# Weighting and adding the early gathered expert rows on ScalarE and GpSimd, with half as many early steps more

## The reference

```python
best_s, sel = lax.top_k(cand_s..., PEER_TOPK)      # 16 of 256 candidates, 8 heads
gate = jax.nn.softmax(best_s, axis=-1)
act = jax.nn.gelu(jnp.einsum('thkd,td->thk', exp_u[idx], xb))
w = gate * act
return jnp.einsum('thk,thkd->td', w, exp_v[idx])
```

## Time and profile before

| | us |
|---|---|
| median of 3 runs | 3281.06 (3277.91 to 3286.41) |
| the profiled execution | 3273.5 |
| its span in the trace | 3271.7 |

### The profile page before, as it was taken

One profiled execution on the slowest core, in us unless ns is written; L12 is line 12 of the kernel. 1 busy time (PEld: TensorE's weight loads), 2 busy tenths in 40 slices (PEclk: granted clock), 3 DMA queues, 4 the chain that ended last, 5 costly groups with the idle time before them and its releaser, 6 DMA issues.

```text
span 3271.7 us, 46700 instructions
## 1 busy us (share of the span) xinstructions
PE 2966.7 (91%) x17310; PEld 2586.0 (79%) x17310; DVE 2489.2 (76%) x5433; ACT 808.7 (25%) x2386; POOL 1050.3 (32%) x840
## 2 busy tenths in 40 slices
PE   6898979999999999976878978789999999999876
PEld 5787868988888888865666856679888888888755
DVE  4277797888888888887543776888888888888876
ACT  3332222212111111211344353122121111111111
POOL 4542112333333333343255421123433323333331
PEclk9999989999999999988978978889999999999888
DMA  4336677899999999999421356668999999999994
GB/s 156 96 101 245 256 262 282 339 421 422 422 422 419 420 414 418 408 421 419 162 68 46 102 180 251 241 249 316 413 422 421 422 419 418 420 416 416 408 422 197
DMA packets 159967, 1042.99 MB, mean 319 GB/s; under 512 B 18480, under 2 KB 23920, under 8 KB 44096
## 3 DMA queue, kind: packets, MB, share of 16 engines
q0 software_dynamic: 92160, 671.13, 50.4%
q1 hardware_dynamic: 63648, 357.59, 28.1%
q10 hardware_dynamic: 4000, 12.36, 1.1%
HBM read 1033.28 MB, written 7.86 MB: 318 GB/s over the span
## 4 chain that ended last, share of the span: by engine, by line
DMA 42%; PE 37%; DVE 11%; issue 8%; ACT 1%; POOL 1%; SPq 0%; DVEq 0%; ACTq 0%; POOLq 0%
DMA gata<-uvg,idxg 25%; DMA gatb<-uvg,idxg 16%; PE bank L711 9%; PE bank L515 8%; DVE acc L1593 5%; PE bank L502 3%; PE bank L724 3%; PE bank L503 3%; PE bank L504 3%; PE bank L698 3%; PE bank L532 1%; PE bank L600 1%; PE bank L856 1%; DVE gata L1585 1%; DVE xf L1355 1%
## 5 line engine op out<-in xcount | busy, mean ns | idle before, releaser
L724 PE MATMUL bank<-a,V 128*128 128x256 f32 x4096 | 949.8, 392 | 100.2 <-DVE a L1576 100.2
L724 PEld LDWEIGHTS bank<-a,V 128*128 128x128 f32 x4096 | 806.8, 198 | 227.1 <-issue 109.9
L711 PE MATMUL bank<-xd,U 128*128 128x256 f32 x4096 | 939.1, 389 | 0.8 <-DMA U<-uvd 0.8
L1266 POOL DMA_INDIRECT gata<-uvg,idxg x428 | 521.6, 1219 | 1247.3 <-DVE acc L1593 1190.2
L711 PEld LDWEIGHTS bank<-xd,U 128*128 128x128 f32 x4096 | 789.4, 195 | 108.4 <-DMA U<-uvd 1.3
L1585 DVE CUSTOM_DVE_ANT_0 gata<-gata,xrow 128x1024 f32<-128x1024 f32 x428 | 522.7, 1222 | 209.3 <-DMA gata<-uvg,idxg 205.6
L1593 DVE SCALAR_TENSOR_TENSOR acc<-gata,wgt,acc 128x1024 f32<-128x1024 f32 x428 | 548.3, 1281 | 30.5 <-ACT wgt L1074 30.4
L1072 ACT ACTIVATE act<-dot 128x1 f32<-128x1 f32 x640 | 129.1, 202 | 1529.7 <-DVE dot L1585 1529.7
L1266 POOL DMA_INDIRECT gatb<-uvg,idxg x212 | 251.8, 1188 | 561.7 <-DVE acc L1593 552.4
L1585 DVE CUSTOM_DVE_ANT_0 gatb<-gatb,xrow 128x1024 f32<-128x1024 f32 x212 | 258.9, 1221 | 110.0 <-DMA gatb<-uvg,idxg 108.8
L698 PEld LDWEIGHTS bank<-B,oneA 128*128 128x128 f16 x4096 | 279.8, 150 | 21.3 <-issue 10.4
(11 more groups left out here) (193 smaller groups left out, 2526.1 us busy)
## 6 DMA issues: line engine op xcount, KB each, us to landing
U<-uvd SPq DMA_DIRECT2D x128, 1024.0 KB, 9.0
V<-uvd SPq DMA_DIRECT2D x128, 1024.0 KB, 9.1
raw<-lin SPq DMA_DIRECT2D x152, 512.0 KB, 3.6
gata<-uvg,idxg POOLq DMA_INDIRECT x428, 14.6
hsp<-h ACTq DMA_DIRECT2D x2, 2304.0 KB, 13.3
hx<-hsp SPq DMA_DIRECT2D x2, 2304.0 KB, 16.5
gatb<-uvg,idxg POOLq DMA_INDIRECT x212, 14.7
sk_g<-skT ACTq DMA_DIRECT2D x2, 1024.0 KB, 4.9
```

The costliest lines, as they stand in the source:

```text
L711: mm = pe.matmul(bank[s][:, TD * t:TD * t + TD], U[:, s, o:o + P], xd[:, k, :], start=(t == 0 and k == 0), stop=(k == DT - 1), skip_group_ ...
L724: mm = pe.matmul(bank[b][:, TD * (d % 2):TD * (d % 2) + TD], V[:, s, o:o + P], a[:, s, TD * k:TD * k + TD], start=(first and k == 0 and d ...
L1266: pool.indirect_dma_start(row(l, s), None, uvg[l], bass.IndirectOffsetOnAxis(idxg[:, s:s + 1], 0)).then_inc(g_in[s % SLOTS], 16)
```

## The change

In front of the builds the addition leaves DVE. For the first SIDE[l] steps (all early ones but the "hot" ones) ACT, once it has the weight, also multiplies the V half by it in place, and POOL adds the result to `acc`. DVE keeps the dot product. POOL's addition of step s - 6 stands directly ahead of its gather of step s. From step SIDE on everything is as before; DVE's first addition waits until POOL's last is done.

The counts change too: 29 steps ahead of the "hot" places become 44 in layer 0, and 33 become 46 in layer 1. `EARLY` is 66 and 68. The loop's first 48 pairs keep 4.5 steps each, so the last 14 pairs have 38 steps where there were 53, and 36 where there were 49.

```diff
 AT = (
-    [("mid1", 3), ("two", 3), ("mix", 1), *[(f"add{m}", 1) for m in range(6)], ("mid2", 2), *[(f"top{m}", 1) for m in range(8, HP)],
-     ("sel3", 3), ("sel4", 3), *[(f"hot{m}", 1 + (m % 4 == 0)) for m in range(LEAD)]],
-    [*[(f"att{n}", 1) for n in range(1, 16, 2)], *[(f"add{m}", 1) for m in range(6)], ("mid1", 3),
+    [("mid1", 4), ("two", 4), ("mix", 3), *[(f"add{m}", 2) for m in range(6)], ("mid2", 3),
+     *[(f"top{m}", 1) for m in range(8, HP)], ("sel3", 5), ("sel4", 5), *[(f"hot{m}", 1 + (m % 4 == 0)) for m in range(LEAD)]],
+    [*[(f"att{n}", 1) for n in range(1, 16, 2)], *[(f"add{m}", 2) for m in range(6)], ("mid1", 4),
      *[(f"top{m}", 1) for m in range(8, HP)],
-     ("sel2", 2), ("sel3", 3), ("sel4", 3), *[(f"hot{m}", 1 + (m % 4 == 0)) for m in range(LEAD)]])
+     ("sel2", 4), ("sel3", 5), ("sel4", 5), *[(f"hot{m}", 1 + (m % 4 == 0)) for m in range(LEAD)]])
 EARLY = tuple(sum(n for _, n in a) for a in AT)
+SIDE = tuple(sum(n for p, n in a if p[:3] != "hot") for a in AT)
...
                 act.activation(wgt[:, k:k + 1], act8[:, k:k + 1], ACT.Copy, scale=gateg[:, s:s + 1])\
                     .then_inc(wgt_done, 1)
+                if s < SIDE[l]:
+                    v = row(l, s)[:, D:RD]
+                    act.wait_ge(wgt_done, NSTEP * l + s + 1)
+                    act.activation(v, v, ACT.Copy, scale=wgt[:, k:k + 1]).then_inc(vw_done, 1)
...
+            def axpy(l, s):
+
+                n = min(s // P, 2)
+                pool.wait_ge(vw_done, SIDE[0] * l + s + 1)
+                if s == 0:
+                    pool.wait_ge(acc_zero, l + 1)
+                pool.wait_ge(ax_done, NSTEP * l + s)
+                pool.tensor_tensor(acc[:, n, :], acc[:, n, :], row(l, s)[:, D:RD], ALU.add).then_inc(ax_done, 1)
+
...
                 for s in range(SLOTS, NSTEP):
+                    if s - SLOTS < SIDE[l]:
+                        axpy(l, s - SLOTS)
                     if s % P == 0:
                         pool.wait_ge(gsel_done, len(GC) * l + s // P + 1)
...
             def gathered(l, s):
 
                 dot_x(l, s)
-                if s == 0:
-                    dve.wait_ge(acc_zero, l + 1)
-                else:
+                if s > SIDE[l]:
                     axpy(l, s - 1)
```

More of the change, by code:

```diff
@@ L297, in program @@
         gsel_done = sem("gsel_done")
+        vw_done = sem("vw_done")
         acc_zero, dot_done, act_done, wgt_done, ax_done = (
```

## The result

| | before | after |
|---|---|---|
| median of 20 runs, us | 3276.91 (3267.63 to 3289.27) | 3287.52 (3278.83 to 3294.18) |
| ratio | | 1.0032 (1.0021 to 1.0043) |
| profiled execution, its span | 3273.5, 3271.7 | 3285.4, 3283.6 |

The kernel became 0.3% slower, where the forecast was 3227 with 3192 to 3272. Both the sign and the range were wrong.

The account below looks back on a forecast made before the run. DMA was taken to bound the pair loops and their ends, PE and DVE by turns the fronts. Ends -70.6 us, fronts +15 and +1, gave -54: from 3281 to 3227 us, range 3192 to 3272.

Parts of the forecast that it names:

- The ends of the loops: Last 14 pairs of both loops: 28 fewer steps at 2.52 us of transfer each, -70.6 us, 60 as other bound.
- The locks: Fronts: POOL's additions block DVE instructions with two SBUF inputs, 2.1 us each, 5 and 4 on the path: +10, +9.
- "add": Output projection places: two steps each outrun POOL's ring, one row per 3.9 us: +8 us per layer (4 to 12).
- "mid1" and "two": Layer 0 front: eight steps with six slots, late rows hold ACT and the statistics behind it: +7.4 us.
- What the front sheds: Fronts: DVE drops 62 additions (79 us), gains 28 dot products (34 us); counts only where DVE sets the pace.
- top places: "top" places in the fronts: a place shrinks from 4.67 to 3.4 us, then PE's scores bound it: -10 us per layer.
- -4.7 at "sel3" and "sel4": "sel3": 10.8 us becomes 6.1, without a wait for ACT's weight, -4.7 per layer; "sel4" was put at 0.
- att: Layer 1's attention: eight additions fewer on DVE, at most -10 us, mostly taken by ACT's multiplication and locks: -4.
- ACT's multiplication: Fronts: 1.05 us each ahead of copies PE waits for, and an idler PE gets less clock: +3 us per layer.
- Case 4: Fronts: every POOL addition blocks DVE's path for 2.1 us, 189 us in all, giving 3397; chance 0.09.
- Case 5: Loop ends don't shorten, since something other than bytes paces them, and fronts still pay 16: 3297; chance 0.05.
- Case 3: POOL's ring also delays rows at "sel3", "sel4" and first "hot" places: +32 us, 3259; chance 0.14.

Follow-up runs that it names:

- writes on POOL: Changed kernel with two memsets, as long as POOL's addition, in that addition's place; those steps stay out of the sum: 3234.69 us, ratio 0.9866.
- no addition: Changed kernel with a no-op in place of POOL's addition; the first 44 and 46 steps stay out of the sum: 3220.08 us, ratio 0.9829.
- the engines alone: Changed kernel with the step counts of the kernel before, so ACT and POOL serve the first 29 and 33 steps: 3273.7 us, ratio 0.9982.

## Why the prediction was wrong

The gain at the ends came as forecast. What failed is the cost in the fronts, 75.6 us where +16 stood: above all the count of locks between DVE and POOL, 9 on the path for +19 us, where the runs show 49.0.

The same marks, as shifts against before counted from the first gather of the layer, in us (worked out from the starts and ends of the instructions named). They show where in the fronts the time comes in:

| | first tile of the output projection | last tile | first write of `xd` | "top0" | "top15" | masks of the fourth chunk | pair 0 |
|---|---|---|---|---|---|---|---|
| layer 0, after | +22.0 | +33.6 | +36.2 | +44.4 | +41.9 | +46.1 | +41.8 |
| layer 0, writes on POOL | +8.7 | +18.5 | +20.7 | +24.6 | +18.5 | +13.6 | +13.8 |
| layer 0, no addition | +5.4 | +12.3 | +14.4 | +19.1 | +13.4 | +8.7 | +10.1 |
| layer 1, after | +2.8 | +14.4 | +16.6 | +24.5 | +21.4 | +29.6 | +33.8 |
| layer 1, writes on POOL | +3.3 | +12.9 | +15.2 | +17.5 | +11.3 | +6.9 | +12.8 |
| layer 1, no addition | +3.9 | +9.7 | +11.9 | +13.1 | +6.9 | +1.7 | +4.3 |

- **The ends of the loops, right.** -70.6 was forecast with 60 as the other bound, -68.4 came. Two windows of after, layer 0 and layer 1, show DMA near 1 as in before:

```profile
1440.00:1583.00 143.00, 117.01 (x474) 96.95 (x472) 106.91 (x138) 21.02 (x84) 44.89 (x37) 0.90 0.97 401
3103.00:3238.00 135.00, 109.95 (x455) 91.91 (x454) 101.00 (x131) 19.89 (x79) 42.78 (x35) 0.92 0.98 405
```

- **The locks, the term that failed.** +19 was forecast, 49.0 measured (28.0 in layer 0 against 10, 21.0 against 9). The price was nearly right, 1.73 us in the mean against 2.1. The count was not: 9 on the path were expected out of 90 additions, while 53 instructions of DVE were blocked, and 49.0 is a little over half of their 91.7 us. It had nothing for the other direction, POOL's gathers that wait for DVE. And three parts of the count fell. It overlooked the normalisation of `uv_d` and `xd` behind the steps, which kept DVE for 7.92 and 7.83 us instead of 3.25; by the first tile of the output projection layer 0 is 13.3 us behind the kernel with writes (22.0 - 8.7), the largest single piece. It took `choose` as mostly searches, but the difference of the first two lines of each layer grows there, from 23.4 to 32.5 and from 10.1 to 22.7. And it let the dot products at "add" fall between additions; four of them took 2.56 to 3.44.
- **"add", near in size, with one bound missed.** +8 was forecast for each layer, with 4 to 12 as bounds, for POOL's ring. From the first to the last tile after takes 11.6 us more in each layer, with writes on POOL 9.8 and 9.6, without the addition 6.9 and 5.8. So the ring bounds there as forecast, at up to 4.64 us a round instead of 3.9, but more than half of the forecast 8 is there without it. The term took it that DMA has room, by the share of the whole front, 0.74, where the stretch itself has 0.89 in before. Six steps more are 6 x 2.52 = 15 us of transfer in a stretch of 27 with 3 to spare.
- **"mid1" and "two", right.** Dot product 7 was to end at 320 in before's time. It ends at 327.82 + 1.78 = 329.60 in after, 320.2 once the 9.4 us ahead of the first gather are taken off. The statistics behind it begin 7.5 us later than in before, where +7.4 was forecast; without POOL's addition it is 4.3. DVE waits 8.91 and 2.50 us for these rows, and PE waits 12.04 for ACT's gelus behind them, as the timelines of DVE and PE show:

```profile
323.71 1.60 DVE L1602 CUSTOM_DVE_ANT_0 gata<-gata,xrow 128x1024 f32<-128x1024 f32 x1 [8.91 <-DMA gata<-uvg,idxg]
327.82 1.78 DVE L1602 CUSTOM_DVE_ANT_0 gata<-gata,xrow 128x1024 f32<-128x1024 f32 x1 [2.50 <-DMA gata<-uvg,idxg]
```

```profile
332.13 1.22 PE L534 MATMUL bank<-g,ones 128*128 128x256 f32 x2 [12.04 <-ACT g L902]
```

- **What the front sheds, half right.** -10 at the top places in each layer became 5.7 and 6.2 without POOL's addition ("top0" to "top15" in the table), and 2.5 and 3.1 in after, where locks stand among them. The -4.7 at "sel3" and "sel4" came without the addition (4.7 and 5.2) and turned into +4.2 and +8.2 with it. So the mechanism is there, and the locks eat it. "att" shed nothing: -4 was forecast, and layer 1's first tile of the output projection comes 2.8 to 3.9 us late in all three kernels of the table.
- **ACT's multiplication.** 1.15 us for each, against 1.05. It costs 10.8 us; the prediction had +6 in its own term and a part of the -4 in "att". Without the multiplication "att" sheds 3.0 us, so it is what turned that sign.

The locks missed by 30 us. The rest of the fronts missed by 26.6 - (16 - 19) = 29.6, and that is no single term. By the rows with writes on POOL it is 7.3 at "att", 7.7 at the top places (6.1 and 6.2 shed instead of 10), 10.7 between the last tile and "top0", for which the prediction had nothing, 3.4 at "add" and 5.9 in layer 1's "hot" places, less the 6 that stood for ACT. Single traces differ by some us where nothing was changed (the stretch between the layers lasts 343.7 to 350.1 us in the twelve), so the small ones among these are not shown.

The rivals. Case 4 had the right mechanism and stood at 9 in 100, but at 189 us it took each addition as 2.1 us on the path; measured are 23 of 90 in its unit (49.0 / 2.1), too few for its own turning point of 40. The point itself was also wrong: without any lock the sum was -54 - 19 = -73 us, and the kernel with writes shows -42 (3234.69 against 3276.79), so half as many locks are enough to turn the sign. Case 5 gave 3297, near the result, by a mechanism that did not happen. Case 3 did not come: in after no dot product behind the "add" places waits over 0.9 us for its row. The range was too narrow since too many locks and a front that sheds less stood as separate cases and never together.

Of the signs, those for the ends (143.2 and 136.3 us), for the loop's pairs and for the waits for rows ("two", and from "add3" on) came as written, and so did the longest dot product, 3.44 us. Pair 0 came 41.8 us later in layer 0 instead of 15. The sign of case 4, a median of the dot products of 2 us or more, did not show the locks: it stayed at 1.22, since a few long instructions of several kinds carry them.

## What to carry to other kernels

- An elementwise operation moved from VectorE to GpSimd is not off VectorE if it reads SBUF while VectorE works on two SBUF tensors. List every such instruction in the stages where the moved one will run, normalisations and masks too, and ask of each whether it has cover. Here the cost was a little over half of the time in blocked instructions, and POOL's gathers waited for DVE as well. The move paid for 62 additions, and no longer for 90.
- Before more transfers are put into a stage, read DMA's share in that stage and not in the larger stretch around it, and sum its free time against the bytes. Of the places tried the best was the one where a step costs the front least, 1.0 us ("hot"), and it was used up after 16 steps.

## What the runs showed that was not expected

- Two memsets of 128x1280 and 128x1344 on POOL keep it as long as the addition (2395 ns against 2404) and leave DVE's instructions with two SBUF tensors alone: 6.4 us in long instructions instead of 91.7, all in casts and scalings.
- A short instruction can lose more than the addition lasts: line 1411's 0.42 us became 3.23, 2.81 in excess of its own, beside an addition of 2.34. It starts at 355.69, ahead of the addition's recorded start at 356.29, and ends 0.3 us behind its end. POOL's gather, 355.31 to 356.27, was running when it began. Whether that holds it until the addition starts was not tried; without the addition no DVE instruction is long beside these gathers.
- Twelve executions fall into two groups by the time ahead of the first gather, 277 and 285 to 286, with the same instructions there, and the clock after a short idle stretch of PE is what differs (1.00 against 0.50 from 120 us on). That stretch is 4.06 us long in all twelve; in the seven it begins at 105.0 to 106.3 us of the span, in the five at 106.6 to 107.7. The ten times of the engines alone also lie in two groups, four from 3261.7 to 3265.1 and six from 3273.0 to 3277.5, and the profiled one, 3263.39, has 277. That speaks for a choice that each execution makes by itself, not for one by the kernel's code; it was not tried.
